# Constant products in the router's gaps on TensorE, and the residual products spread over the first four experts

## The reference, cut to what matters

```
for layer in range(2):
    mix = mamba2_mixer(h, ...) if layer == 0 else diff_attention(h, ...)
    h = layer_norm(ALPHA * h + mix, g_mix, b_mix)
    ffn = hier_moe(h, w_group, w_expert, w_gate, w_up, w_down)
    h = layer_norm(ALPHA * h + ffn, g_ffn, b_ffn)

# hier_moe, per token: the best of 4 groups, in it the best 2 of 8 experts
g_sel = argmax(softmax(x @ w_group));  top_p, top_i = top_k(softmax(x @ w_expert of that group), 2)
y = sum over the 2 experts of weight * ((silu(x @ w_gate[e]) * (x @ w_up[e])) @ w_down[e])
```

## Time and profile before

| | |
|---|---|
| timed runs, median (lowest, highest) | 2253.1 us (2251.59, 2255.76) |
| profiled execution, first to last instruction | 2257.6 us |
| TensorE busy | 2090.0 us, 93% |
| VectorE, ScalarE, GpSimd busy | 745.3, 364.6, 86.5 us |
| mean granted TensorE clock | 0.895 of full |
| read from HBM | 562.14 MB, 249 GB/s over the span |
| router and experts of layer 0, start of `pe_route(0)` to end of the last combine | 293.7 to 776.0 us |
| the same of layer 1 | 953.1 to 1431.3 us |

### The profile page before, as it was taken

One profiled execution on the slowest core, in us unless ns is written; L12 is line 12 of the kernel. 1 busy time (PEld: TensorE's weight loads), 2 busy tenths in 40 slices (PEclk: granted clock), 3 DMA queues, 4 the chain that ended last, 5 costly groups with the idle time before them and its releaser, 6 DMA issues.

```text
span 2257.6 us, 32970 instructions
## 1 busy us (share of the span) xinstructions
PE 2090.0 (93%) x13605; PEld 1401.4 (62%) x13605; DVE 745.3 (33%) x2250; ACT 364.6 (16%) x968; POOL 86.5 (4%) x92
## 2 busy tenths in 40 slices
PE   8999999998888798999998888897999999799998
PEld 7687576765655444576666565444688544458863
DVE  4354242221212315522222222467222115733211
ACT  2222110100000113210000000114221001322100
POOL 0112100000000100000000000000001000000110
PEclk9999977988888897777878888997999999889999
DMA  9333459999999952469999999941344344214420
GB/s 338 130 113 120 146 204 402 424 423 425 425 425 423 401 207 82 147 263 425 426 424 424 424 425 424 340 150 38 120 154 150 126 149 152 73 62 172 149 93 19
DMA packets 112382, 565.33 MB, mean 250 GB/s; under 512 B 12456, under 2 KB 15726, under 8 KB 79470
## 3 DMA queue, kind: packets, MB, share of 16 engines
q1 hardware_dynamic: 112238, 563.21, 63.1%
HBM read 562.14 MB, written 1.05 MB: 249 GB/s over the span
## 4 chain that ended last, share of the span: by engine, by line
PE 86%; DVE 5%; DMA 4%; issue 4%; ACT 1%; SPq 0%; DVEq 0%; ACTq 0%
PE ps L2434 14%; PE ps L669 11%; PE ps L1633 11%; PE ps L650 10%; PE ps L295 9%; PE ps L708 7%; PE ps L1200 5%; DMA ring<-in_moe_w_up_dram 4%; PE ps L761 3%; PE ps L1306 3%; PE ps L1210 2%; PE ps L690 2%; PE ps L1976 1%; PE ps L1719 1%; DVE tiny L1806 1%
## 5 line engine op out<-in xcount | busy, mean ns | idle before, releaser
L2434 PE MATMUL ps<-arena,ring 128*128 128x256 f32 (+1 forms) x1536 | 305.5, 362 | 0.0
L2434 PEld LDWEIGHTS ps<-arena,ring 128*128 128x128 f32 x1536 | 271.9, 190 | 33.9 <-issue 1.0
L650 PEld LDWEIGHTS ps<-arena 128*128 128x128 f32 x2048 | 247.2, 201 | 27.6 <-issue 26.6
L1633 PE MATMUL ps<-ring,arena 128*128 128x512 f32 (+1 forms) x576 | 251.1, 595 | 3.8 <-DVE arena L420 3.8
L650 PE MATMUL ps<-arena 128*128 128x32 f32 x2048 | 254.0, 285 | 0.0
L669 PE MATMUL ps<-ring,arena 128*32 128x256 f32 x2816 | 189.1, 424 | 46.0 <-issue 35.8
L295 PE MATMUL ps<-ring,arena 128*128 128x512 f32 x480 | 211.9, 602 | 0.8 <-ACT arena L2277 0.8
L1633 PEld LDWEIGHTS ps<-ring,arena 128*128 128x128 f32 x576 | 109.9, 193 | 136.4 <-issue 136.1
L669 PEld LDWEIGHTS ps<-ring,arena 128*32 128x32 f32 x2816 | 112.8, 123 | 122.8 <-issue 86.9
L295 PEld LDWEIGHTS ps<-ring,arena 128*128 128x128 f32 x480 | 92.5, 194 | 115.3 <-issue 113.6
L2494 DVE SCALAR_TENSOR_TENSOR arena<-ps,pcol,arena 128x255 f32<-128x255 f32 (+1 forms) x176 | 84.8, 482 | 210.8 <-ACT arena L2467 207.7
(11 more groups left out here) (306 smaller groups left out, 1974.6 us busy)
## 6 DMA issues: line engine op xcount, KB each, us to landing
ring<-in_moe_w_gate_dram SPq DMA_DIRECT2D x44, 2048.0 KB, 29.5
ring<-in_moe_w_up_dram SPq DMA_DIRECT2D x44, 2048.0 KB, 33.9
ring<-in_moe_w_down_dram SPq DMA_DIRECT2D x44, 2048.0 KB, 30.4
ring<-in_w_up_dram SPq DMA_DIRECT2D x22, 2048.0 KB, 8.1
arena<-in_moe_w_gate_dram SPq DMA_DIRECT2D x20, 2048.0 KB, 29.2
arena<-in_moe_w_up_dram SPq DMA_DIRECT2D x20, 2048.0 KB, 33.7
arena<-in_moe_w_down_dram SPq DMA_DIRECT2D x20, 2048.0 KB, 31.1
ring<-in_ssm_w_in_dram SPq DMA_DIRECT2D x12, 2048.0 KB, 9.8
```

Source lines behind the costliest of these rows:

```text
L650: mm = nc.tensor.matmul(ps[:, 4, k * CAP:(k + 1) * CAP], normed[:, tt, k, :], slots[:, b, tt, :], start=(tt == 0), stop=(tt == TT - 1))
L1633: mm = nc.tensor.matmul(ps[:, bank + n % 4, 0:n_cols], xT[:, k, tt * P:(tt + 1) * P], w[:, k, :], start=(k == 0), stop=(k == KD - 1))
L2434: mm = nc.tensor.matmul(ps[:, n % 4, lo:hi], w[:, k, k4 * P:(k4 + 1) * P], xT_mlp[:, k, lo:hi], start=(k == 0), stop=(k == KD - 1))
```

## The change

The change does three things, in both layers alike. It takes the 16+8 residual products out of the router and puts constant products of 512 columns in their place: 4 before the second transposes, 2 between these and `pe_route(1)`, 3 between `pe_route(1)` and `pe_counts`. They go to bank 5; the one that stood before the experts stays and goes to bank 4 as before. It does all 32 residual products in the first four experts, 8 behind each `step_down` (experts 0 and 1 for token tile 0, experts 2 and 3 for tile 1). And it moves the experts' rows `y` from the arena to `h[:, 1, :]`, since `xT_route` is now read for longer.

```
-        def pe_stay_awake(pe, n):
+        def pe_stay_awake(pe, bank, n):
             for _ in range(n):
-                nc.tensor.matmul(ps[:, 4, :], ident, cst[:, C_TRIU:C_TRIU + 512], start=True, stop=True)
+                nc.tensor.matmul(ps[:, bank, :], ident, cst[:, C_TRIU:C_TRIU + 512], start=True, stop=True)
...
-            y = area(0, D)
+            y = h[:, 1, :]
...
                     if peeled and e == 0:
                         head.pe_tally(pe)
-                        head.pe_residual(pe, 1, range(4, KD))
...
                     step_down(pe, m, v, before, b, w[2])
+                    if peeled:
+                        head.pe_residual(pe, i // 2, range(i % 2 * 4, i % 2 * 4 + 4))
                     if i == 1:
                         step_back_turn(pe, m, m["back"].at(q + 1), 4)
...
             head0.pe_route(pe, 0)
-            head0.pe_residual(pe, 0, range(KD))
+            pe_stay_awake(pe, 5, 4)
             pe_turn_normed(pe, 1)
+            pe_stay_awake(pe, 5, 2)
             head0.pe_route(pe, 1)
-            head0.pe_residual(pe, 1, range(4))
+            pe_stay_awake(pe, 5, 3)
             head0.pe_counts(pe)
-            pe_stay_awake(pe, 1)
+            pe_stay_awake(pe, 4, 1)
             experts0.pe(pe)
```

More of the change, by code:

```diff
@@ L1994, in pe_attention1 @@
             head1.pe_route(pe, 0)
-            head1.pe_residual(pe, 0, range(KD))
+            pe_stay_awake(pe, 5, 4)
             pe_turn_normed(pe, 1)
+            pe_stay_awake(pe, 5, 2)
             head1.pe_route(pe, 1)
-            head1.pe_residual(pe, 1, range(4))
+            pe_stay_awake(pe, 5, 3)
             head1.pe_counts(pe)
-            pe_stay_awake(pe, 1)
+            pe_stay_awake(pe, 4, 1)
             experts1.pe(pe)
```

## The result

The changed kernel took 2241.5 us (median of 5 runs, 2236.0 to 2243.7) against 2252.3 us (5 runs, 2251.0 to 2255.8), a ratio of 0.995 with a 95% interval of 0.9934 to 0.9965. In a second job it took 2236.6 us (9 runs, 2231.8 to 2255.0) against 2251.1, 0.9947 (0.9930 to 0.9965). So the change saves about 11 us, with 8 to 16 in the intervals: half a per cent of the kernel's time.

A forecast was written before the change was run, and what follows sets the result against it. The prediction took the stream of weight loads to bound the expert stages. Earlier stream start (-7.8, -4.5), load 2 (-3.5, -1.5) and later loads (+2.5 each layer) gave -12.3 us, from 2253.1 to 2241 us; range 2232 to 2252.

The forecast's parts named there:

- The bound: Expert stages: the stream of weight loads sets them; a stage ends a fixed time after its start, plus every gap.
- The start of the stream: Router to first expert's gate/up: constants hold the clock; weight loads start 7.8 us earlier in layer 0, 4.5 in layer 1.
- The transposes: Router: by the skill page's rule, transposes don't engage the full clock; the forecast held that the trace contradicts this.
- rival C: Router: the clock falls in spite of the constants, each then costing 1.85 us; +5 us, 2258 us; chance 0.08.
- Load 2: Weight load released by the first expert's down: no longer late, gaining 3.5 us in layer 0 and 1.5 in layer 1.
- The loads behind it: Later weight loads, first experts: moved residual products make them 2.5 us late in each layer (ends 0 and 10.3).
- rival D: First four experts: residuals at half clock behind each down keep gate/up at low clock; +23 us, 2276 us; chance 0.04.
- The sum: Both layers: -8.8 us in layer 0 and -3.5 in layer 1, together -12.3 us, giving 2241 us.

The follow-up runs named there:

- only the wait filled: The kernel before, plus two constant products between the second transposes and the second route, nothing moved: 2239.4 us against 2251.1, 0.9959.
- the late residual products: The changed kernel with four bank-clearing products for three router constants and all 32 residual products behind the downs of experts 28 and 29: 2239.4 against 2248.5 us.

## Why the prediction was right

**The bound.** Right in the main. D to the last combine is 445.4 to 451.6 us in all 27 readable stages, while D itself moves from 24 to 36.5 us. But the prediction called this part fixed, and its width of 6 us is as much as the change gains in a layer. In two of the longest (451.6 us, and 450.2 in layer 0 with only the wait filled) the clock fell in the last experts and no wait for weights was left there; for the others with 449 us and more the cause was not looked for, but for the late residual products.

**The start of the stream.** Right, and shown by the runs with and without constants. Forecast for layer 0: second route at full clock to 303.9 (303.8), counts from 306.4 on (306.25), pick at 308.1 (307.8) in 3.9 us (3.76), gate/up 5.5 (4.96). Load 0 came 8.8 us earlier, forecast 7.8. In layer 1 it is 23.0 us behind the first route instead of 29.7: 6.7 us, forecast 4.5, mainly since the gate/up products took 3.66 us where I put 5.5.

**The transposes.** The Trainium skill's page (TensorE: Matmul & The Clock Gate, Part 4: PE-mode transpose) would have led to rival C. No stage with all constants in the router lost the clock before the pick: the second route took 1.95 us or less in every one of them. So the time that I worked out from the page did not come. What is not tested is the page's sentence by itself: the eight transposes last 1.1 us between constants, and no run has a long stretch of transposes alone.

**Load 2.** Right on the issue times: it is 0.3 us late in the first changed trace where it was 3.5 and 1.5 before, and the latest load is now load 3, 1.6 us late, for which the prediction had no row. As a gain in time the term is not shown: moving that group alone changed neither the time nor the stages' ends.

**The loads behind it.** Near in the mean, wrong as a description. I put one value, 2.5 us late in each layer, which was 1.4 too little. The six stages show 1.6, 1.5, 9.8, 1.5, 7.4 and 1.4, a mean of 3.9. There are two cases: in one the clock stays up behind the downs and the residual products cost little, in the other they and the gate/up products run at half clock. I had given this (rival D) 0.04 as a case for the whole kernel; it is an event of single stages, in two of six, both in layer 0 and both in executions that were the slowest of nine, so its share in usual ones is likely smaller. It may also be what gives single runs of the changed kernel their width; no trace of a run in the middle was taken to show that.

**The sum.** The forecast for D was 27.7 us in both layers (36.5 - 8.8 and 31.2 - 3.5), the mean of the six stages is 28.0. Three errors offset each other: load 0 earlier than I said in layer 1, later loads later, and the profile of before being a long one in layer 0 (D 36.5, 33.2 in the next), which the prediction suspected. That the time came within 1 us of 2241 is in part luck beyond that: the six stages gave 5.6 us of the forecast 12.3, and the traces have another 4.6 in the second model, on which the prediction had no term. A slip in rival C (985.1 in layer 1, where its own terms give 985.8) bears on nothing, nor does the PE row of the slices shown at the start, which has three digits too many; the page has `8999999998888798999998888897999799799998`.

**Which part of the change.** The prediction priced constants and moved products together. The runs show the first: without the nine constants nothing is left of the gain, and two of them in one wait, with nothing moved, gained as much as the intervals can tell. That the other seven, or moving the residual products, add anything is not shown. Moving `y` is not shown to cost anything (2250.3 against 2250.0 us in the experiment that moved it without constants).

## What to carry to other kernels

In a stage that is bound by a stream of loads, look for the first release and the latest release, and put work that must be done behind the instruction that releases a slot. Narrow matmuls cost twice here: by themselves, and by the clock of the wide ones behind them; the same 32 products in another place cost the whole gain, while moving fewer of them gained nothing that the runs can tell. Try the smallest form first: two constant products in one wait did as much as the whole change. Where the clock's fall decides, single executions differ by more than the change, and two profiles of each kernel are needed before any difference between stages is explained.

## What was not expected of the hardware

Useless wide products made the kernel faster: in one job the changed kernel took 0.9947 of the time before, and the same without its nine constants 1.0011, which is 14 us more, though TensorE has 8.4 us a layer less to do (3.68 + 1.88 + 2.82). And in one stage 8 products of 64 columns took 2.00 us behind expert 1's down and 3.68 behind the other three, and the 64 records behind them 3.66 or 6, the same instructions on the same shapes, in stretches at full and at half clock. Nor is the clock a fixed property of a program: the second model, which no version here touches, took 818.0 to 826.3 us in single executions, and the two longest are those with a low clock in both of the places shown.
